# The expert values of three token blocks as dense products with the whole value table, started when the coefficients of all three blocks are complete

## What is computed

```python
N_EXPERTS = 128 * 128; PEER_HEADS = 8; PEER_TOPK = 16
def block(hb):                                   # 128 tokens
    q = (hb @ w_query).reshape(TOK_BLOCK, PEER_HEADS, 2, D_QHALF)
    sc = jnp.einsum('thpc,pnc->thpn', q, sub_keys)
    ...                                          # two top-16, then the top-16 of their 256 sums
    idx = jnp.take_along_axis(cand_i, best_j, axis=-1)
    gate = jax.nn.softmax(best_s, axis=-1)
    u = expert_u[idx]
    act = jax.nn.gelu(jnp.einsum('thkd,td->thk', u, hb), approximate=False)
    coef = (gate * act)
    return jnp.einsum('thk,thkd->td', coef, expert_v[idx])
```

## Time and profile before

| what | value |
|---|---|
| time, median of 3 runs | 3862.79 us (3862.74 to 3863.1) |
| the profiled execution, first to last instruction | 3861.4 us |
| PE busy | 2869.3 us (74%) |
| DVE busy | 2555.5 us (66%) |
| ACT busy, POOL busy | 612.4 us, 1603.5 us |
| moved by DMA | 1508.29 MB, mean 391 GB/s |
| first dot product of the stream | 633.61 us |

### The profile page before, as it was taken

The page is one execution under the profiler, slowest core; times in us unless marked ns, Lnnn a source line. Parts: engine busy times, 40 slices in busy tenths (PEclk is TensorE's granted clock), DMA queues, the critical chain, the costliest instruction groups (busy, mean ns, idle before and its releaser), DMA issues.

```text
span 3861.4 us, 27082 instructions
## 1 busy us (share of the span) xinstructions
PE 2869.3 (74%) x8298; PEld 1204.2 (31%) x8298; DVE 2555.5 (66%) x3844; ACT 612.4 (16%) x1438; POOL 1603.5 (42%) x1163
## 2 busy tenths in 40 slices
PE   4999997989999865777779789755555555555555
PEld 1333443743334332333333355411111111111111
DVE  3110215886788787555556777899898998777676
ACT  0000201121121122233310111211111111000011
POOL 3000001444333454333333454456546656665654
PEclk7999998989999988888889799877677777777778
DMA  9999556999999999999999999999999999999998
GB/s 308 398 359 369 209 185 254 405 415 412 412 411 410 404 420 416 419 419 419 419 406 410 409 383 413 418 415 419 417 415 403 400 417 420 420 420 420 420 415 320
DMA packets 275058, 1508.29 MB, mean 391 GB/s; under 512 B 27241, under 2 KB 27241, under 8 KB 116857
## 3 DMA queue, kind: packets, MB, share of 16 engines
q0 software_dynamic: 162208, 1152.39, 72.9%
q1 hardware_dynamic: 109202, 334.10, 23.0%
q10 hardware_dynamic: 3504, 20.06, 1.3%
HBM read 1491.81 MB, written 13.80 MB: 390 GB/s over the span
## 4 chain that ended last, share of the span: by engine, by line
DMA 54%; PE 35%; issue 5%; DVE 4%; POOL 2%; ACT 1%; SPq 0%; POOLq 0%; DVEq 0%; ACTq 0%
DMA arena<-in_expert_v_dram,arena 47%; PE ps L945 10%; PE ps L551 7%; PE ps L760 6%; PE ps L710 4%; PE ps L642 3%; POOL arena L2206 2%; DMA arena<-in_w_ada_dram 2%; PE ps L539 2%; DMA arena<-in_w_out_dram 1%; DMA arena<-in_w_query_dram 1%; DMA arena<-in_w_in_dram 1%; DVE arena L1897 1%; PE ps L753 1%; PE ps L509 1%
## 5 line engine op out<-in xcount | busy, mean ns | idle before, releaser
L945 PE MATMUL ps<-arena 128*128 128x512 f32 (+1 forms) x2176 | 1385.0, 774 | 855.8 <-DMA arena<-in_expert_v_dram,arena 835.2
L1958 DVE CUSTOM_DVE_ANT_0 arena<-arena 128x2048 f32<-128x2048 f32 x544 | 1246.3, 2291 | 444.8 <-DMA arena<-in_expert_u_dram,arena 439.7
L2206 POOL DMA_INDIRECT arena<-in_expert_v_dram,arena x544 | 878.7, 1615 | 1113.8 <-PE ps L945 802.4
L945 PEld LDWEIGHTS ps<-arena 128*128 128x128 f32 (+1 forms) x2176 | 450.7, 225 | 1707.3 <-issue 1479.0
L2206 POOL DMA_INDIRECT arena<-in_expert_u_dram,arena x544 | 682.0, 1254 | 578.6 <-DVE arena L1958 339.7
L1897 DVE SCALAR_TENSOR_TENSOR arena<-arena 128x1024 f32<-128x1024 f32 x539 | 691.7, 1283 | 250.8 <-issue 223.7
L760 PE MATMUL ps<-arena 128*128 128x512 f32 x896 | 399.5, 599 | 1.0 <-DVE arena L1850 1.0
L1340 ACT ACTIVATE arena<-arena 128x128 f32<-128x128 f32 (+1 forms) x544 | 205.1, 392 | 1128.6 <-PE ps L945 951.3
L551 PE MATMUL ps<-arena 128*128 128x512 f32 x640 | 289.7, 606 | 8.9 <-DMA arena<-in_w_in_dram 8.9
L760 PEld LDWEIGHTS ps<-arena 128*128 128x128 f32 x896 | 165.6, 190 | 236.3 <-issue 233.6
L710 PE MATMUL ps<-arena 128*128 128x288 f32 (+1 forms) x896 | 215.4, 400 | 3.1 <-DMA arena<-in_w_query_dram 3.1
(11 more groups left out here) (235 smaller groups left out, 1487.1 us busy)
## 6 DMA issues: line engine op xcount, KB each, us to landing
arena<-in_w_ada_dram SPq DMA_DIRECT2D x96, 1024.0 KB, 10.6
arena<-in_w_in_dram SPq DMA_DIRECT2D x80, 1024.0 KB, 14.1
arena<-in_w_query_dram SPq DMA_DIRECT2D x36, 1024.0 KB, 18.3
arena<-in_w_out_dram SPq DMA_DIRECT2D x32, 1024.0 KB, 5.1
arena<-in_cache_k_dram SPq DMA_DIRECT2D x24, 1024.0 KB, 10.4
arena<-in_cache_v_dram SPq DMA_DIRECT2D x24, 1024.0 KB, 20.8
arena<-in_expert_u_dram,arena POOLq DMA_INDIRECT x544, 16.5
arena<-in_expert_v_dram,arena POOLq DMA_INDIRECT x544, 17.0
```

Of the source, the lines that this page charges most:

```text
L945: ins = MM(ps[0:rows, c, :], diag[t % 4][:, 0:rows], value[:, c * NC:(c + 1) * NC], start=(j == 0), stop=last, skip_group_check=True)
L1958: V.tensor_tensor_reduce(out=u_slot[s % RING], in0=u_slot[s % RING], in1=h2[b], scale=1.0, scalar=0.0, op0=ALU.mult, op1=ALU.add, accum_ou ...
L2206: nc.gpsimd.indirect_dma_start(out=slot, out_offset=None, in_=table, in_offset=bass.IndirectOffsetOnAxis(ap=idx, axis=0),).then_inc(loaded ...
```

## The change

The values of blocks 0, 1 and 2 are no longer gathered. Instead a matrix C (16384 experts by 384 tokens) is built that holds each token's coefficient at the experts which it chose, and the sum is the product of C with the whole table `expert_v`.

- For every pair of tokens DVE writes four 128x128 tables (`one_hot`): for each of the token's 128 slots the coefficient at the first key, and a one at the second key. One matmul per token makes its 128x128 coefficients in PSUM, ACT copies them out for four tokens at a time into `stage`, and for every 32 tokens a store of 2 MB goes to `dense_coefs` in DRAM: 192 pairs, 384 matmuls, 96 copies, 12 stores. Their dues: block 0 from step 132, a pair each 1.8 steps; block 1 from 259, each 0.75; block 2 from 386.5, each 0.27, the last at 403.5.
- The table is read in 256 tiles of 128 rows by 1024 columns (0.5 MB, four buffers `dense_v`): first all rows of the low half, then all of the high half. For a tile there are two matmuls 128x512 for each of the three blocks. Sixteen chunks of C (1.5 MB, two buffers) are read for each half. `EARLY_TILES` is 0, so the first chunk's load waits for all 12 stores and the first tile for all 96 copies. The weights of a matmul are `dense_c[...][:, P * b:P * b + P, i % JS]`, every eighth float of a chunk.
- Blocks 3 and SB keep their gathers, but all 2048 columns of a value row are now added by DVE, and PE takes no part. `LAG` is 24 steps. The choices of block 3 are due at 330 to 426, those of SB at 440 to 496.
- The three blocks' residual rows are loaded back (`reload`). At step 470 DVE closes the low halves (`end_low`), the high halves after the last step. PE has no stream loop any more: it runs `side.upto(END)` at once, then folds the samples' sums.

```diff
-LAG = GRP + 3
+LAG = 3 * GRP
...
+DENSE = 3
...
+JS = 8
...
+V_DENSE = 4
+EARLY_TILES = 0
...
+    return order + [(1, i, everyone) for i in range(NKEY)]
...
+C_FROM = [131.0, 258.0, 385.5]
+C_STEP = [1.8, 0.75, 0.27]
...
+def t_pair(b, g):
+    return C_FROM[b] + 1.0 + C_STEP[b] * g
...
+            def build_dense():
+                for b in range(DENSE):
+                    yield C_FROM[b] + 0.4
+                    pe.wait_ge(coef_done, SLOTS // GRP * (b + 1))
+                    pe.wait_ge(keys_split, b + 1)
+                    if b:
+                        pe.wait_ge(quad_taken, QUADS * b)
+                    for i, src in enumerate((gate_all[:, b, :], slot_keys[:, 0, :], slot_keys[:, 1, :])):
+                        ins = TT(ps[:, 0, i * P:(i + 1) * P], src, ident)
+                    ins.then_inc(slots_turned, 1)
+                    for g in range(PAIRS):
+                        yield t_pair(b, g) + 0.2
+                        n = PAIRS * b + g
+                        quad = n // 2
+                        pe.wait_ge(hot_ready, n + 1)
+                        if g % 2 == 0 and quad >= 2:
+                            pe.wait_ge(quad_taken, quad - 1)
+                        for i in range(2):
+                            at_col = (2 * (g % 2) + i) * P
+                            ins = MM(ps[:, quad % 2, at_col:at_col + P], one_hot[n % 2][:, i, 1, :], one_hot[n % 2][:, i, 0, :],
+                                     start=True, stop=True, skip_group_check=True)
+                        ins.then_inc(hot_used, 1)
+
+            def tile_of_block(m, b):
+                half, i, _ = TILES[m]
+                weights = dense_c[CHUNK_OF[m] % 2][:, P * b:P * b + P, i % JS]
+                for c in range(2):
+                    ins = MM(ps[:, BANK[half, b] + c, :], weights, dense_v[m % V_DENSE][:, c * NC:(c + 1) * NC],
+                             start=(m == FIRST_TILE[half, b]), stop=(m == LAST_TILE[half, b]), skip_group_check=True)
+                return ins
...
+            def tile_loaded(m):
+                u = CHUNK_OF[m]
+                pe.wait_ge(c_loaded[u % 2], 16 * (u // 2 + 1))
+                pe.wait_ge(dv_loaded[m % V_DENSE], 16 * (m // V_DENSE + 1))
...
+            def dense():
+                for m in range(N_LOW):
+                    yield t_tile(m)
+                    if m == 0:
+                        pe.wait_ge(quad_taken, QUADS * (DENSE - 1))
+                        pe.wait_ge(scb_copied, 6 * PH)
+                        pe.wait_ge(qry_copied, 4 * PH - 2)
+                    if m == EARLY_TILES:
+                        pe.wait_ge(quad_taken, QUADS * DENSE)
+                    tile_loaded(m)
+                    for b in TILES[m][2]:
+                        ins = tile_of_block(m, b)
+                    ins.then_inc(tile_used, 1)
+                yield t_tile(N_LOW)
+                for b in range(DENSE):
+                    if b:
+                        pe.wait_ge(low_free, 2 * b)
+                    for m in range(N_LOW, N_LOW + V_DENSE):
+                        tile_loaded(m)
+                        ins = tile_of_block(m, b)
+                        if b == DENSE - 1:
+                            ins.then_inc(tile_used, 1)
+                for m in range(N_LOW + V_DENSE, len(TILES)):
+                    tile_loaded(m)
+                    for b in range(DENSE):
+                        ins = tile_of_block(m, b)
+                    ins.then_inc(tile_used, 1)
...
-            for s in range(END + LAG):
-                t = s - LAG
-                if t >= 0:
-                    b, j = STREAM[t]
...
-                    pe.wait_ge(diag_done, t + 1)
-                    value, loaded, n_loaded = value_home(t)
-                    pe.wait_ge(loaded, n_loaded)
-                    for c in range(2):
-                        ins = MM(ps[0:rows, c, :], diag[t % 4][:, 0:rows], value[:, c * NC:(c + 1) * NC],
-                                 start=(j == 0), stop=last, skip_group_check=True)
-                    ins.then_inc(v_done, 1)
-                side.upto(s)
-            pe.wait_ge(scb_copied, 6 * PH)
...
-            pe.wait_ge(add_done, END)
-            for c in range(2):
...
+            side.upto(END)
+            pe.wait_ge(add_done, END - GATHERED)
+            pe.wait_ge(low_free, 2 * DENSE)
+            pe.wait_ge(fin_sq[1], 2)
+            for i in range(2):
+                if i:
+                    pe.wait_ge(fin_x[1], 2)
+                for c in range(2):
+                    ins = MM(ps[0:NS, c, :], sel, acc[:, i * HALF + c * NC:i * HALF + (c + 1) * NC], start=True, stop=True)
+                ins.then_inc(acc_folded, 1)
...
+                    for q in range(QUADS):
+                        yield t_pair(b, 2 * q + 1) + 0.4
+                        n = QUADS * b + q
+                        part, at_t = n // 8, 4 * (n % 8)
+                        act.wait_ge(hot_used, 2 * n + 2)
...
+                        A.copy(stage[part % 2].rearrange("p c t j -> p t c j")[:, at_t:at_t + 4, :, :],
+                               ps[:, n % 2, :].rearrange("p (t c j) -> p t c j", t=4, j=JS)).then_inc(quad_taken, 1)
+                        if n % 8 == 7:
+                            act.wait_ge(quad_taken, n + 1)
+                            act.dma_start(c_dram[:, :, part, :].rearrange("c p x -> p c x"),
+                                          stage[part % 2].rearrange("p c t j -> p c (t j)")).then_inc(stage_stored[part % 2], 16)
...
+                    for g in range(PAIRS):
+                        yield t_pair(b, g)
+                        n = PAIRS * b + g
+                        if g == 0:
+                            dv.wait_ge(slot_t_done, b + 1)
+                            dv.wait_ge(keys_split, b + 1)
+                        if n >= 2:
+                            dv.wait_ge(hot_used, n - 1)
+                        for i in range(2):
+                            t = 2 * g + i
+                            V.tensor_scalar(one_hot[n % 2][:, i, 0, :], iota_key, slot_t[:, 1, t:t + 1], slot_t[:, 0, t:t + 1],
+                                            ALU.is_equal, ALU.mult)
+                            ins = V.tensor_scalar(one_hot[n % 2][:, i, 1, :], iota_key, slot_t[:, 2, t:t + 1], None, ALU.is_equal)
+                        ins.then_inc(hot_ready, 1)
...
+                    dv.wait_ge(fin_x[1], 1)
                 if j == 0:
-                    V.tensor_scalar(acc, half, scale, None, ALU.mult).then_inc(add_done, 1)
+                    V.tensor_scalar(acc, value, scale, None, ALU.mult).then_inc(add_done, 1)
                 else:
-                    V.scalar_tensor_tensor(out=acc, in0=half, scalar=scale, in1=acc, op0=ALU.mult, op1=ALU.add).then_inc(add_done, 1)
+                    V.scalar_tensor_tensor(out=acc, in0=value, scalar=scale, in1=acc, op0=ALU.mult, op1=ALU.add).then_inc(add_done, 1)
+
+            def end_half(half, b):
+                for c in range(2):
+                    cols = slice(half * HALF + c * NC, half * HALF + (c + 1) * NC)
+                    sums = ps[:, BANK[half, b] + c, :]
+                    link(V.tensor_tensor(sums, sums, gate2_kept[:, cols], ALU.mult))
+                    ins = V.tensor_tensor(h2[b][:, cols], h2[b][:, cols], sums, ALU.add)
+                    if half == 0:
+                        ins.then_inc(low_free, 1)
+                    else:
+                        ins.then_inc(fin_x[0], 1)
+
+            def end_low():
+                yield T_LOW
+                dv.wait_ge(tile_used, N_LOW)
+                dv.wait_ge(x1_back, 48)
+                dv.wait_ge(kept_loaded, 32)
+                for b in range(DENSE):
+                    end_half(0, b)
+
...
                     coefs(s // GRP - 1)
-                for b in range(BLOCKS):
+                for b in range(DENSE, BLOCKS):
                     finish(b, s)
...
+                if GATHERED <= s - LAG < END:
                     add(s - LAG)
                 side.upto(s)
+            dv.wait_ge(tile_used, len(TILES))
+            for b in range(DENSE):
+                end_half(1, b)
+            for b in range(DENSE):
+                mean(b)
+            for b in range(DENSE):
+                scale_rows(b)
...
+            def load_chunk(u):
+                half, i, blocks = TILES[CHUNK_AT[u]]
+                parts = slice(4 * blocks[0], 4 * blocks[-1] + 4)
+                if u >= 2:
+                    sp.wait_ge(tile_used, CHUNK_AT[u - 1])
+                for n in range(2):
+                    sp.wait_ge(stage_stored[n], 8 * 4 * (blocks[-1] + 1))
+                sp.dma_start(dense_c[u % 2][:, GRP_T * parts.start:GRP_T * parts.stop, :].rearrange("p t j -> p (t j)"),
+                             c_dram[i // JS, :, parts, :].rearrange("p g x -> p (g x)")).then_inc(c_loaded[u % 2], 16)
...
+            def load_tile(m):
+                half, i, _ = TILES[m]
+                if m >= V_DENSE:
```

(14 more changed lines are left out.)

384 lines of the change are left out of this document (219 added, 165 removed).

## The result

The changed kernel takes 3907.39 us (median of 4 runs), the kernel before 3862.76 us: a ratio of 1.012, 95% interval 1.0106 to 1.0134. It is slower, where the forecast was 3836 and faster.

What follows compares the result with a forecast made beforehand. DMA bounds the kernel before; after the change each stretch's largest load does. 633.5 + 1814 puts the last pair at 2447 us, first tile 2475, PE's 1318 ends at 3793, plus 38 is 3831; forecast 3836, own range 3800 to 3870.

Steps and rivals of the forecast that it cites:

- rival (1): Up to the last pair: slower than its largest loads, PE and DVE tied by pairs; at 6%, 3945 us; chance 0.24.
- the prediction's own signs of being wrong: Tiles wait for their loads, tile records stand over 0.43 us apart, or the last pair comes after 2500 us.
- The part up to the complete C: Up to the last pair: each stretch's largest load plus a little for waits, sum 1814 us, last pair at 2447.
- steps 111 to 143: The attention's stretch: DVE 71 + 34 + 6 for pairs; 120 us with waits in the attention's chain.
- steps 33 to 111: First projection: PE 341 us as first bound, DMA 306, DVE 290; 345 us taken.
- steps 143 to 203: Before the second projection: DMA 323 us with three stores of C, DVE 206; 340 us taken.
- Last pair to first tile: Reload, twelfth store and chunk load ahead of the first tile: 28 us, first tile at 2475 us.
- The tiles: 256 tiles, 3072 PE records at 0.429 us: 1318 us, PE hardly ever waiting, ending at 3793 us.
- rival (3): In the tiles: strided weight loads aren't hidden; at 0.50 us a record 215 us more, 4050; chance 0.05.
- The wait of DVE for tile 128: At step 470 DVE waits 150 to 200 us, ending near 3134 us; costs nothing while later gathers fit.
- Rival (2): Gathers after step 470 don't fit; stream ends 10 to 40 us after PE, 3850 to 3880; chance 0.10.
- The end: From PE's end to the span's end: samples' fold and norm, high-half operations, last store; 38 us, ending at 3831.

Runs made afterwards that it cites:

- att_wide: Changed kernel with attention heads 5.0 instead of 3.75 steps apart and samples 5.35 instead of 6.6: 3888.06 us, ratio 1.0058 to the kernel before.
- proj_less: Changed kernel without two of block 3's four matmuls in each quarter of both projections: 3849.01 us, ratio 0.996 to the kernel before.
- barrier494: Changed kernel with DVE turning to the low halves at step 494 instead of 470: 3913.88 us, ratio 1.0131 to the kernel before.
- early64_b458: Changed kernel with 64 early tiles and DVE turning to the low halves at step 458 instead of 470: 3874.15 us, ratio 1.0028 to the kernel before.

## Why the prediction was wrong

The mechanism that it named was right: 197 MB less on DMA were not turned into time, because the products stand alone behind the last pair, and PE's 1318 us follow there. Its sign was wrong because of sizes. The outcome is rival (1)'s, at 3.4% and not 6%, and so are the prediction's own signs of being wrong: the last pair came at 2509, after its 2500, and some tiles waited for their loads. On the span of 3903.3 us against 3835:

**The part up to the complete C**: +61 us, the step that failed. It is the rule "the largest load, with a little for waits": the loads were right, the waits beside them were not. Three things were in it.
First, steps 111 to 143 were sized by DVE's work, 111 us, with 9 for waits; they took 153, not 120. DVE's work was 110 us, its waits 44: 39 of them for the attention's matmuls, and 17 of these for the first head, which starts behind PE's wait for `out_dram`. The heads' dues count in steps, and a step that no longer waits for 2 MB can pass in 2.2 us and not in 5.4, so the chain of a head no longer has dot products enough to hide behind. att_wide showed a part of it: wider spacing takes 27 us off that stretch and 12 off the time up to step 203.
Second, DMA's load was divided by 415 GB/s, which the rows of before show with u and v gathers together. With u gathers alone DMA was busy 0.98 of steps 307 to 330 at 381 GB/s, and with the weights' loads beside them 0.95 at 370 in proj_less; both are 389 GB/s for a full share. So DMA's load of steps 33 to 111 was nearer to PE's 349 us than the 306 of the sum: 124 MB at 389 GB/s are 319 us, an estimate.
Third, where the loads stand within 20% of each other, the stretch is longer than the largest: 365 us for PE's 349, 161 for DVE's 131, 180 for 155 and 152. proj_less shows how soft such a bound is: of the 96 us of PE work taken away from two such stretches, 39 came off. How much of this is the second point and how much in-order waiting wasn't separated. What rival (1) names, DVE waiting for pairs, is the smaller part. DVE's waits in the whole part, for rows of `expert_u` and for pairs:

```profile
DVE arena L2156 <- DMA arena<-in_expert_u_dram,arena: 143.7, 93, 8.4
DVE arena L2052 <- PE ps L1016: 24.4, 20, 9.4
```

Half of the first line, 73 us, lies in steps 143 to 203, where DMA is full. The rest of DVE's waits there are for other side work: the choices' exponentials on ACT, the projections, the attention. So the time is rival (1)'s, and its named cause explains 24 us of waits at most; whether the stops of the gathers that it also names count for more wasn't tried.
Against all this, steps 143 to 203 were 37 us better than the sum: 126 MB at 417 GB/s are exactly their 303 us. 20 of the 37 are bytes, since two stores of C fall into them and not three, and 17 were put on for waits and not needed. Steps 386.5 to 404 were 12 us better: DVE waited 4.9 us for pairs, where 11 stood for PE's low clock, which did come (0.54).
One working of the prediction doesn't follow from its text: with 3.41 us a step the side work of steps 111 to 143 would be 39 us. Its 34 follow from 3.58, the two busy times and the earlier trace rows, and the measured 110 us bear out the 34.

**Last pair to first tile**: 20 us for 28.

**The tiles**: 1339 us for 1318. The record's 0.429 us was right to the third digit, and the strided weights are hidden, so rival (3) was rightly small. "PE hardly ever to wait" cost 18 us in two places, 11 of waits for loads and most of the rest by the clock behind them.

**The wait of DVE for tile 128**: 189 us, ended at 3197; 150 to 200 was forecast, and that it costs nothing is shown by barrier494. The DMA margin behind it was enough: the stream's last add ended 26 us before PE's last tile. Rival (2) didn't come about, but it was near, and in early64_b458 it is seen.

**The end**: 35.5 us for 38, and the 4 us for late gathers weren't needed. The terms: 61 - 8 + 21 - 2 - 4 = 68 us.

That the first part's length goes into the time nearly one to one is shown twice: 13 us off the last pair and 13 off the span in att_wide, 44 and 50 in proj_less. Of the 662 us that the forecast wanted to win by the last pair, 3109 - 2447, 600 were won; from there to the end of the span it takes 1394 us, where it took 752 from step 404 before. The margin of the forecast was 27 us on a sum of fifteen terms, which came out between 0 and 37 us off; a chance of 0.24 for rival (1) was too low, and it decided from 20 to 25 us on, by the prediction's own account.

## What to carry to other kernels

When a bound of one resource is taken away, the dues, spacings and lookaheads that were set in units of its steps come apart: read again what each chain hides behind when a step takes half the time. Where engines and DMA stand near each other, expect more than the largest load (here 4% to 23% in four stretches), and don't trust a forecast of the sign whose margin is under that. Work that has to wait for a complete intermediate result should be split so that its first part fills the engine that idles ahead of it, only until the other resource is full (here 32 of the low half's 128 tiles, 3907 to 3850 us), and it costs whoever waits for what then stands behind it in the same list; and a wait that looks like a loss can be what keeps unurgent transfers away from urgent ones.

## What the runs showed of the hardware

Weight loads of 128x128 fp32 took 191 ns from neighbouring floats and 314 ns from floats 32 bytes apart.

DMA moved 381 GB/s at a share of 0.98 where it carried almost only row gathers from `expert_u` (steps 307 to 330) and 370 at 0.95 with the projections' weights beside them, but 417 at 1.01 with the samples' cache beside them and 415 at 1.01 with tile loads and gathers from both tables: 389 against 411 to 413 for a full share. Why a byte costs more in the first two wasn't tried.

Gathers on POOL's queue took DMA from the tile loads that PE waited for: with 64 early tiles, 12 steps of gathers more or less moved the low half's end by 50 us each way (3122, 3172 and 3222 us).

PE's granted clock was 0.50, the lower level, while PE had nothing to do (2211 to 2391 us), still 0.54 with the pairs' small matmuls, and 0.99 in the tiles; the first tile took 7.5 us instead of 5.15. It was 0.50 again for some 5 us behind two waits for loads of 3.8 and 4.0 us inside the tiles (2725 to 2730 and 3230 to 3235 us). With 64 early tiles in the stretches before the last pair the clock was 0.74 to 0.86.
